# A residual block in split precision: another order of the eleven weight slabs of a pair, other places for the side work, and one more weight sum made by a DMA

## The chip, the cores and the metric

The kernel runs on one core of a Trainium2 chip. The metric is the time of one execution on the device, in microseconds (us); the median of three runs is given. Engines: TensorE (PE; PEld are its weight loads), VectorE (DVE), ScalarE (ACT), GpSimd (POOL) and SyncE (SP). SP issues the plain DMA loads, POOL the DMAs that add to what is in the buffer.

## What is computed

One layer over 256 positions of width 2048, in float32:

```
h = RMSNorm(x);  p = h @ W_in                      # 2048 -> 7168
A = retention over 8 heads (rotary, decay, group norm, gate)
B = chunked attention over 8 heads (QK norm, relative bias)
x = x + concat(A, B) @ W_out                       # 2048 -> 2048
h = RMSNorm(x)
x = x + square(relu(h @ W1)) @ W2                  # 2048 -> 8192 -> 2048
```

The change is in the last line, the feed-forward part.

## The kernel before, in words

**Split precision.** Each float32 weight slab (128 partitions x 2048 elements, 1 MB: four blocks of 128 rows by 512 columns) is split in two halves of the matmul's type: ScalarE copies the raw slab to `w_hi` (`hi_slab`, line 904), VectorE subtracts `w_hi` from the raw slab into `w_lo` (`lo_slab`, line 1244). The activations are split the same way into *forms* (`hF_hi`/`hF_lo` for the up projection, `dF_hi`/`dF_lo` for the down projection). A block product is then three matmuls of 512 columns: hi x hi, hi x lo, lo x hi. `w_hi` and `w_lo` are rings of three slabs, so `hi_slab(s)` waits until the matmuls have used slab s-3 (`slab_used`), and the matmuls of slab s wait for `slab_lo`.

**Fewer products.** The part runs as four rounds; in each, 2048 hidden values are made (up) and used (down). A round has four *pairs* (line 675): two of kind U (up, each with two column groups of 512) and two of kind D (down). Half of the inner dimension of a pair is done by a seven-product scheme instead of eight (sums and differences of blocks of weights and of activations): the steps Q1, P5, P6, Q2, P7, P3, P4, each a `product` of 12 matmuls. The other half is done plainly: the four steps R1 to R4 (`rest`), each of 24 matmuls on one slab. The R steps of a pair are run one pass later, between the products of the next pair; pass p has eleven steps:

```
STEPS = 11
R1, Q1, R2, P5, R3, P6, R4, Q2, P7, P3, P4 = range(STEPS)
```

After P4 comes R1 of the next pass, so the four products Q2, P7, P3, P4 stand in a row.

**Weight sums.** P5, P6, P7 and P4 need sums of the four raw slabs a, b, d and e of the pair. a is read by Q1. Then VectorE adds b to a (`sum_slabs`, line 1252) for P5, and d to it for P6. POOL's DMAs add from HBM: one adds d's weights to the buffer of b (line 453) for P7, released by the first VectorE sum; one adds e's to the buffer of a (line 457) for P4, released by P6's low half. Plain loads of d and e serve P3 and Q2.

**Results.** The products lie in the PSUM banks bX, bF, bH, bY, bZ, bW. `keep_q1` (ScalarE, line 955) copies Q1's result out of bX before P6 may write there; `sum_u1`, `sum_u2`, `sum_u3`, `sum_v4` (VectorE, lines 1350 to 1366) form the partial results. For a U pair the next pass adds them to the banks (`up_sum`, into `hid`), applies ReLU and square on ScalarE (lines 943, 948), and TensorE transposes the hidden values in two halves (`hid_blocks`, line 672; eight transposes each). From them `stage`, `d_mix_of`, `d_hi` and `d_lo` make the eleven forms of the down projection: seven from the first U pair, four from the second. For a D pair `add_products` and `add_bank` add to `xs`, the running x.

**Order.** Nothing is planned at run time: every engine has its list written out by hand in its loop over p, with the side work placed between two slabs. All waits are semaphore counts. The raw slabs lie in five buffers; `raw_plan` (line 303) gives each load the buffer whose last reader comes first, and SP issues the loads in the order of `sources` (line 289), each behind the low half that reads the buffer last (`slab_lo`, line 408).

Of the kernel before, what the change touches and what calls it, by code (L numbers as in the profile page):

```python
# [56 lines left out]
R1, Q1, R2, P5, R3, P6, R4, Q2, P7, P3, P4 = range(STEPS)  # L57
# [7 lines left out]
def hybrid_block(nc, x, x_cols, w_att, w_ret, w_out, w_up, w_down, gains, rel_windows, rope_cos, rope_sin, decay, out):  # L65
# [3 lines left out]
    with ExitStack() as ctx:  # L69
# [176 lines left out]
        b_summed = sem("b_summed")  # L246
        e_summed = sem("e_summed")
# [102 lines left out]
        def added(p):  # L350

            return 2 * OUT_GROUPS + 4 * (2 * (p // 4) + p % 4 - 2)

# [4 lines left out]
        def _(sp):  # L358
# [54 lines left out]
            for c in range(4):  # L413
                for m in range(MT):

                    sp.wait_ge(acc_read_dve, added(PAIRS - 2 + c // 2) + 2 * (c % 2) + m + 1)
                    sp.dma_start(out_rows[:, m, c * N:(c + 1) * N], xs[:, m, c * N:(c + 1) * N]).then_inc(stored, 16)
# [4 lines left out]
        def _(pool):  # L422
# [48 lines left out]
        def _(pe):  # L471
# [148 lines left out]
            def rest(p, step, hi, lo, form, banks, opens, closes):  # L620
# [4 lines left out]
                for m in range(MT):  # L625
# [7 lines left out]
                    if closes and m == 0:  # L633
                        mm.then_inc(half_used, 1)
                mm.then_inc(slab_used, 1)
# [39 lines left out]
            for p in range(PAIRS + 1):  # L675
# [6 lines left out]
                def forms(n):  # L682

                    if up:
                        pe.wait_ge(hF_lo_ok, n)
                    else:
                        pe.wait_ge(dF_lo_ok, FORMS * g + n)
# [9 lines left out]
                else:  # L697
                    rest_forms(9)
                    rest(p, R1, hi_, lo_, REST, (bH, bY), (False, False), False)
                if live:  # L700
                    forms(1)
# [9 lines left out]
                if live:  # L711
                    forms(3)
# [8 lines left out]
                if live:  # L721
                    forms(6)
# [8 lines left out]
                if live:  # L731
                    forms(7)
                    bank_read(pe, prev, 0)
                    product(p, Q2, hi, lo, A12, bH, False)
                    pe.wait_ge(u1_ok, p + 1)
                    product(p, P7, hi, lo, S3N, bX, True)
                    bank_read(pe, prev, 2)
                    product(p, P3, hi, lo, S4, bZ, False)
                    if was_up:
                        hid_blocks(prev, 1)  # L740
                    if prev < 0:
                        x_blocks(OUT_GROUPS - 1)
                    bank_read(pe, prev, 1)
# [4 lines left out]
        def _(act):  # L748
# [135 lines left out]
            def hi_slab(s):  # L884
# [5 lines left out]
                if step in (P5, P6):  # L890
                    act.wait_ge(summed, 2 * p + (P5, P6).index(step) + 1)
# [58 lines left out]
            def keep_q1(p):  # L950

                act.wait_ge(slab_used, slab_no(p, Q1) + 1)
                if p > 0:
                    bank_read(act, p - 1, 0)
                nc.scalar.activation(q1[:], bX[:], ACT.Copy).then_inc(q1_ok, 1)

            def stage(u, n):

                act.wait_ge(hid_tr, 8 * (u // 4) + n + 1)
                nc.scalar.activation(sd[:, n, :], bT[n % 2][:], ACT.Copy).then_inc(d_stage, 1)  # L960
# [8 lines left out]
            for p in range(PAIRS + 1):  # L969
                prev, s = p - 1, STEPS * p  # L970
                was_up, first_up, live = kind(prev) == "U", prev >= 0 and prev % 4 == 0, p < PAIRS
                if not live:
# [7 lines left out]
                if prev % 4 == 1 and prev >= 0:  # L980
                    act.wait_ge(d_mix, 4 * (prev // 4) + 2)
                    d_hi(S1, sd[:, 1, :])
                    d_hi(A12, sd[:, 2, :])
                    d_hi(A22, sd[:, 3, :])

                hi_slab(s + 3)
                if prev % 4 == 1 and prev >= 0:
                    act.wait_ge(d_mix, 4 * (prev // 4) + 3)
                    d_hi(S2N, sd[:, 0, :])
# [5 lines left out]
                if prev % 4 == 1 and prev >= 0:  # L995
                    act.wait_ge(d_mix, 4 * (prev // 4) + 4)
                    d_hi(S4, sd[:, 2, :])

                hi_slab(s + 5)
                keep_q1(p)  # L1000

                hi_slab(s + 6)
                if was_up:
# [5 lines left out]

                hi_slab(s + 7)  # L1010

                hi_slab(s + 8)
                if first_up:
                    stage(prev, 0)
# [5 lines left out]
                hi_slab(s + 9)  # L1020
                if was_up:
                    relu(prev, 0, 1)
                    relu(prev, 1, 1)
                    square(prev, 0, 1)
                    square(prev, 1, 1)
                if first_up:
                    d_hi(A11, sd[:, 0, :])

                hi_slab(s + 10)
                if p == 0:  # L1030
                    stream_squares(OUT_GROUPS - 1)
                if first_up:
                    act.wait_ge(d_mix, 4 * (prev // 4) + 1)
                    d_hi(S3N, sd4[:])

                hi_slab(s + 11)

                hi_slab(s + 12)
                if first_up:
                    stage(prev, 2)  # L1040
                    stage(prev, 3)
                elif was_up:
                    d_rest(prev, 2)
                    d_rest(prev, 3)
# [3 lines left out]
        def _(dve):  # L1048
# [283 lines left out]
            def add_products(p, m, second):  # L1332
# [4 lines left out]
                dve.wait_ge(ready, p + 1)  # L1337
                nc.vector.tensor_tensor(cols, other[:], cols, ALU.add).then_inc(xs_ok, 1)

            def add_bank(p, m, second):  # L1340
# [4 lines left out]
                if p >= 0:  # L1345
                    dve.wait_ge(xs_ok, added(p) - 2 * OUT_GROUPS + 2 * second + m + 1)
# [3 lines left out]
            def sum_u1(p):  # L1350

                dve.wait_ge(slab_used, slab_no(p, P6) + 1)
                dve.wait_ge(q1_ok, p + 1)
                nc.vector.tensor_tensor(u1[:], bX[:], q1[:], ALU.add).then_inc(u1_ok, 1)
# [20 lines left out]

            for p in range(PAIRS + 1):
                prev, s = p - 1, STEPS * p
                kept, live = kind(prev), p < PAIRS
                first_up = prev >= 0 and prev % 4 == 0
                second_up = prev >= 0 and prev % 4 == 1  # L1380
                g = prev // 4
                if not live:
# [4 lines left out]
                    for second in range(2):  # L1387
                        for m in range(MT):
                            add_products(prev, m, second)
                    for second in range(2):  # L1390
                        for m in range(MT):
                            add_bank(prev, m, second)
# [4 lines left out]
                else:  # L1397
                    sum_u2(prev)
# [5 lines left out]
                if second_up:  # L1404
                    dve.wait_ge(d_stage, 4 * g + 4)
                    d_mix_of(sd[:, 1, :], sd[:, 1, :], sd[:, 3, :], ALU.subtract)
                    d_lo(g, 3, S1, sd[:, 1, :])

                lo_slab(s + 3)
                if p > 0:  # L1410
                    sum_v4(prev)
                if second_up:
                    d_lo(g, 4, A12, sd[:, 2, :])
                    d_lo(g, 5, A22, sd[:, 3, :])
                    dve.wait_ge(d_mix, 4 * g + 2)
                    d_mix_of(sd[:, 0, :], sd[:, 1, :], sd[:, 0, :], ALU.subtract)

                sum_slabs(p, "a", "d", ["d"])
                lo_slab(s + 4)
# [3 lines left out]
                if second_up:  # L1423
                    d_lo(g, 6, S2N, sd[:, 0, :])
                    dve.wait_ge(d_mix, 4 * g + 3)
                    d_mix_of(sd[:, 2, :], sd[:, 2, :], sd[:, 0, :], ALU.add)
                if kept == "D":
                    add_products(prev, 0, 0)
                    add_products(prev, 1, 0)

                lo_slab(s + 5)
                if second_up:
                    d_lo(g, 7, S4, sd[:, 2, :])
                if kept == "U":
                    up_sum(prev, 0, 0)
                    up_sum(prev, 1, 0)
                if kept == "D":
                    add_bank(prev, 0, 0)
                    add_bank(prev, 1, 0)

                lo_slab(s + 6)

                lo_slab(s + 7)

                if kept == "D":
                    add_products(prev, 0, 1)
                    add_products(prev, 1, 1)
                sum_u1(p)
                lo_slab(s + 8)
                if kept == "U":  # L1450
                    up_sum(prev, 0, 1)
                else:
                    add_bank(prev, 0, 1)

                lo_slab(s + 9)
                if kept == "U":
                    up_sum(prev, 1, 1)
                else:
                    add_bank(prev, 1, 1)
                if first_up:  # L1460
# [79 lines left out]
```

## Time and profile before

| | us |
|---|---|
| median of three runs | 1175.92 (1172.63 to 1175.97) |
| the profiled execution, its own time | 1176.99 |
| its span | 1175.0 |
| TensorE busy | 1124.2 |
| VectorE busy | 888.5 |
| ScalarE busy | 632.8 |
| mean granted TensorE clock | 0.988 of full |
| HBM read | 250.37 MB |

A busy time is the time in which the engine has an instruction under way; the matmuls overlap each other by some tenths of a microsecond, so a busy TensorE may still be slowed. The feed-forward part begins near 421 us and ends with the span; the first D pair of the second round is the pass called pair 6 (passes count from 0). In the timeline a row is: start, length, engine, line, operation, output<-inputs, shapes, count, and in brackets how long the engine had been idle and what released it.

### The profile page before, as it was taken

What the parts mean: (1) busy time and instruction counts of PE and PEld (TensorE: products, weight loads), DVE (VectorE), ACT (ScalarE), POOL (GpSimd) and SP (SyncE); (2) the same over time, 40 slices, a digit from 0 to 9 for tenths busy, and PEclk for the clock granted to TensorE, in tenths of its full rate; (3) what the DMA queues carried; (4) which work ended last, traced back from release to release, by engine and by line L of the source; (5) the groups of instructions that cost most, each with busy time, mean ns of one, the idle gap of its engine ahead of it and who ended that gap; (6) DMA issues with size and microseconds to landing.
All of it is one profiled execution on the core that took longest, in us unless ns stands there. A gap on an engine that the chain in (4) does not pass through costs nothing.

```text
span 1175.0 us, 13700 instructions
## 1 busy us (share of the span) xinstructions
PE 1124.2 (96%) x5234; PEld 948.8 (81%) x5234; DVE 888.5 (76%) x924; ACT 632.8 (54%) x717; POOL 53.4 (5%) x58
## 2 busy tenths in 40 slices
PE   8999999999999999988999998999998999997998
PEld 8889889989988878776788876788876788876787
DVE  6667667657657678786898877888876889877885
ACT  6545445445454556556555555555565554574652
POOL 0000000000000000100000000000000000000000
PEclk9999999999999999999999998999999999999999
DMA  9745445445455467866688765688866788875692
GB/s 358 303 165 195 161 169 191 166 148 207 165 195 180 179 215 250 231 198 214 193 266 282 228 218 183 213 281 248 238 232 166 224 294 230 265 238 139 232 259 100
DMA packets 39551, 253.14 MB, mean 215 GB/s; under 512 B 4432, under 2 KB 4944, under 8 KB 12624
## 3 DMA queue, kind: packets, MB, share of 16 engines
q1 hardware_dynamic: 34896, 218.93, 50.7%
q0 software_dynamic: 4608, 33.56, 15.4%
q8 instruction: 33, 0.54, 0.2%
q14 instruction: 14, 0.11, 0.0%
HBM read 250.37 MB, written 2.10 MB: 215 GB/s over the span
## 4 chain that ended last, share of the span: by engine, by line
PE 75%; DVE 11%; ACT 8%; issue 3%; DMA 2%; SPq 0%; ACTq 0%; DVEq 0%
PE acc L485 10%; PE acc L487 10%; PE acc L486 10%; PE acc L628 8%; PE acc L631 8%; PE acc L630 8%; DVE w_lo L1244 6%; ACT w_hi L904 5%; PE bankC L614 2%; PE bankC L616 2%; PE bankC L615 2%; PE acc L614 2%; PE acc L616 2%; PE acc L615 2%; DMA raw<-in_w_ret 1%
## 5 line engine op out<-in xcount | busy, mean ns | idle before, releaser
L1244 DVE TENSOR_TENSOR w_lo<-raw,w_hi 128x2048 fp32r<-128x2048 f32 x180 | 411.4, 2288 | 120.9 <-ACT w_hi L904 120.9
L904 ACT ACTIVATE w_hi<-raw 128x2048 fp32r<-128x2048 f32 x180 | 342.3, 1912 | 193.7 <-PE acc L631 120.2
L1051 DVE TENSOR_TENSOR w_lo<-raw,w_hi 128x1024 fp32r<-128x1024 f32 (+1 forms) x152 | 167.6, 1107 | 67.1 <-ACT w_hi L756 67.0
L485 PE MATMUL acc<-w_hi,hT_hi 128*128 128x512 f32 (+1 forms) x512 | 191.6, 374 | 2.9 <-DVE w_lo L1051 2.9
L487 PE MATMUL acc<-w_hi,hT_lo 128*128 128x512 f32 (+1 forms) x512 | 185.7, 363 | 0.0
L486 PE MATMUL acc<-w_lo,hT_hi 128*128 128x512 f32 (+1 forms) x512 | 185.5, 362 | 0.0
L756 ACT ACTIVATE w_hi<-raw 128x1024 fp32r<-128x1024 f32 (+1 forms) x152 | 142.8, 963 | 33.8 <-PE acc L487 27.5
L628 PE MATMUL acc<-w_hi,hF_hi 128*128 128x512 f32 x256 | 103.6, 405 | 15.3 <-DVE w_lo L1244 14.3
L485 PEld LDWEIGHTS acc<-w_hi,hT_hi 128*128 128x128 f32 x512 | 96.3, 188 | 13.2 <-DVE w_lo L1051 3.8
L487 PEld LDWEIGHTS acc<-w_hi,hT_lo 128*128 128x128 f32 x512 | 96.1, 188 | 10.2
L486 PEld LDWEIGHTS acc<-w_lo,hT_hi 128*128 128x128 f32 x512 | 96.4, 188 | 9.5
L631 PE MATMUL acc<-w_hi,hF_lo 128*128 128x512 f32 x256 | 101.9, 398 | 0.0
L630 PE MATMUL acc<-w_lo,hF_hi 128*128 128x512 f32 x256 | 101.6, 397 | 0.0
L628 PE MATMUL acc<-w_hi,dF_hi 128*128 128x512 f32 x256 | 100.0, 391 | 0.1
L630 PE MATMUL acc<-w_lo,dF_hi 128*128 128x512 f32 x256 | 99.7, 390 | 0.0
L631 PE MATMUL acc<-w_hi,dF_lo 128*128 128x512 f32 x256 | 99.6, 389 | 0.0
L1252 DVE TENSOR_TENSOR raw<-raw 128x2048 f32<-128x2048 f32 x32 | 73.0, 2282 | 0.0
L628 PEld LDWEIGHTS acc<-w_hi,hF_hi 128*128 128x128 f32 x256 | 49.5, 193 | 27.8 <-issue 16.5
L631 PEld LDWEIGHTS acc<-w_hi,hF_lo 128*128 128x128 f32 x256 | 49.2, 192 | 10.8
L630 PEld LDWEIGHTS acc<-w_lo,hF_hi 128*128 128x128 f32 x256 | 49.7, 194 | 10.1
L628 PEld LDWEIGHTS acc<-w_hi,dF_hi 128*128 128x128 f32 x256 | 48.2, 188 | 10.9 <-issue 0.9
L631 PEld LDWEIGHTS acc<-w_hi,dF_lo 128*128 128x128 f32 x256 | 48.2, 188 | 10.1
(191 smaller groups left out, 1716.4 us busy)
## 6 DMA issues: line engine op xcount, KB each, us to landing
raw<-in_w_up SPq DMA_DIRECT2D x64, 1024.0 KB, 6.1
raw<-in_w_down SPq DMA_DIRECT2D x64, 1024.0 KB, 5.0
raw<-in_w_ret SPq DMA_DIRECT2D x32, 1024.0 KB, 4.8
raw<-in_w_att SPq DMA_DIRECT2D x28, 768.0 KB, 4.3
raw<-in_w_out SPq DMA_DIRECT2D x16, 1024.0 KB, 4.9
raw<-in_w_up POOLq DMA_DIRECT2D x16, 1024.0 KB, 8.6
raw<-in_w_down POOLq DMA_DIRECT2D x16, 1024.0 KB, 8.8
raw<-in_w_att SPq DMA_DIRECT2D x8, 384.0 KB, 7.2
```

Of the source, the lines that this page charges most:

```text
L485: nc.tensor.matmul(o, hi[:, k, tile_cols(m)], wh, start=first, stop=False)
L486: nc.tensor.matmul(o, hi[:, k, tile_cols(m)], wl, start=False, stop=False)
L487: mm = nc.tensor.matmul(o, lo[:, k, tile_cols(m)], wh, start=False, stop=last)
L614: nc.tensor.matmul(bank[:], hi[:, form, tile_cols(t)], wh[:, cols], start=t == 0, stop=False)
L628: nc.tensor.matmul(banks[m][:], hi[:, form + m, tile_cols(t)], wh[:, cols], start=opens[m] and t == 0, stop=False)
L630: nc.tensor.matmul(banks[m][:], hi[:, form + m, tile_cols(t)], wl[:, cols], start=False, stop=False)
L631: mm = nc.tensor.matmul(banks[m][:], lo[:, form + m, tile_cols(t)], wh[:, cols], start=False, stop=closes and t == SLAB_KT - 1)
L756: nc.scalar.activation(piece(w_hi, q, 0, PIECE_KT * n), raw[:, q // 2, (q % 2) * PIECE_KT * n:(q % 2 + 1) * PIECE_KT * n], ACT.Copy).then_ ...
L904: nc.scalar.activation(w_hi[:, ring(s)], raw[:, r, :], ACT.Copy).then_inc(slab_hi, 1)
L1051: nc.vector.tensor_tensor(piece(w_lo, q, 0, PIECE_KT * n), raw[:, q // 2, (q % 2) * PIECE_KT * n:(q % 2 + 1) * PIECE_KT * n], piece(w_hi, ...
L1244: nc.vector.tensor_tensor(w_lo[:, ring(s)], raw[:, r, :], w_hi[:, ring(s)].bitcast(f32), ALU.subtract).then_inc(slab_lo, 1)
L1252: nc.vector.tensor_tensor(raw[:, r, :], raw[:, r, :], raw[:, q, :], ALU.add).then_inc(summed, 1)
```

## The change

The order of the steps becomes R1, Q1, R2, P5, Q2, R3, P6, R4, P7, P3, P4. In the list of loads e comes before d. The sum for P6 (d added to the buffer of a) is no longer made by VectorE but by a third POOL DMA, released by P5's low half. The second half of a U pair's transposes moves from before P4 to the middle of R1 of the next pass, and with it the side work of ScalarE and VectorE moves to other slabs; the bank is added to x before the first two product sums, and the order of waits follows.

```diff
-R1, Q1, R2, P5, R3, P6, R4, Q2, P7, P3, P4 = range(STEPS)
+R1, Q1, R2, P5, Q2, R3, P6, R4, P7, P3, P4 = range(STEPS)
...
-                order += [(p, "d")] if p < PAIRS else []
+                order += [(p, "e"), (p, "d")] if p < PAIRS else []
                 order += [(p - 1, "R3"), (p - 1, "R4")]
-                order += [(p, "e")] if p < PAIRS else []
...
+        X_FORMS = {Q1: 1, P5: 3, Q2: 4, P6: 6, P7: 6, P3: 7, P4: 7}
+        D_FORMS = {Q1: 1, P5: 3, Q2: 3, P6: 4, P7: 5, P3: 6, P4: 7}
... POOL, add_slabs(p)
-                pool.wait_ge(summed, 2 * p + 1)
+                pool.wait_ge(summed, p + 1)
                 row = ((first + 1) * SLABS + 1) * P
                 nc.gpsimd.dma_start(raw[:, PLAN[p, "b"][0], :], table[row:row + P, :],
                                     accum_op=ALU.add).then_inc(b_summed, 16)
+                pool.wait_ge(slab_lo, slab_no(p, P5) + 1)
+                nc.gpsimd.dma_start(raw[:, PLAN[p, "a"][0], :], table[row:row + P, :],
+                                    accum_op=ALU.add).then_inc(d_summed, 16)
                 pool.wait_ge(slab_lo, slab_no(p, P6) + 1)
... TensorE
-                    rest(p, R1, hi_, lo_, REST, (bH, bY), (False, False), False)
+                    rest(p, R1, hi_, lo_, REST, (bH, bY), (False, False), False,
+                         (lambda: hid_blocks(p - 2, 1)) if kind(p - 2) == "U" else None)
...
+                    forms(Q2)
+                    bank_read(pe, prev, 0)
+                    product(p, Q2, hi, lo, A12, bH, False)
                 if prev < 0:
                     rest_out(R3, 2)
...
-                    if was_up:
-                        hid_blocks(prev, 1)
... ScalarE, hi_slab(s)
-                if step in (P5, P6):
-                    act.wait_ge(summed, 2 * p + (P5, P6).index(step) + 1)
+                if step == P5:
+                    act.wait_ge(summed, p + 1)
+                elif step == P6:
+                    act.wait_ge(d_summed, 16 * p + 16)
... ScalarE, pass p (new list)
                 hi_slab(s + 2)
+                if held_first:
+                    stage(p - 2, 2, A12)
+                    stage(p - 2, 3)
+                if held_second:
+                    d_rest(p - 2, 2)
+                    d_rest(p - 2, 3)
                 hi_slab(s + 3)
+                if held_first:
+                    act.wait_ge(d_mix, 4 * g + 1)
+                    d_hi(S1, sd4[:])
...
+                hi_slab(s + 6)
+                if held_first:
+                    act.wait_ge(d_mix, 4 * g + 3)
+                    d_hi(S2N, sd[:, 0, :])
+                hi_slab(s + 7)
                 keep_q1(p)
                 if was_up:
                     relu(prev, 0, 0)
                     relu(prev, 1, 0)
                     square(prev, 0, 0)
                     square(prev, 1, 0)
+                if held_first:
+                    d_hi(S3N, sd[:, 1, :])
                 hi_slab(s + 8)
+                hi_slab(s + 9)
...
+                hi_slab(s + 10)
                 if was_up:
                     relu(prev, 0, 1)
+                hi_slab(s + 11)
+                if was_up:
                     relu(prev, 1, 1)
+                hi_slab(s + 12)
+                if was_up:
                     square(prev, 0, 1)
                     square(prev, 1, 1)
... VectorE, pass p (new list)
+                    sum_u3(prev)
                     sum_u2(prev)
                 sum_slabs(p, "a", "b", ["b"])
                 lo_slab(s + 2)
+                if p > 0:
+                    sum_v4(prev)
+                if held_first:
                     dve.wait_ge(d_stage, 4 * g + 4)
+                    d_mix_of(sd4[:], sd[:, 1, :], sd[:, 3, :], ALU.subtract)
+                    d_lo(g, 2, A12, sd[:, 2, :])
+                if held_second:
+                    d_lo(g, 10, REST + 2, bT[0][:])
+                    d_lo(g, 11, REST + 3, bT[1][:])
                 lo_slab(s + 3)
-                sum_slabs(p, "a", "d", ["d"])
...
                 lo_slab(s + 4)
+                if p > 0:
+                    read_first(prev)
+                lo_slab(s + 5)
+                if was_down:
+                    add_products(prev, 0, 0)
...
+                lo_slab(s + 7)
+                if was_down:
+                    add_products(prev, 1, 0)
+                    add_products(prev, 0, 1)
+                    add_products(prev, 1, 1)
...
+                lo_slab(s + 8)
                 sum_u1(p)
                 lo_slab(s + 9)
+                for m in range(MT):
+                    up_sum(prev, m, 1) if was_up else add_bank(prev, m, 1)
+                if held_first:
+                    d_lo(g, 6, S4, sd[:, 2, :])
+                    d_lo(g, 7, A22, sd[:, 3, :])
...
```

`held_first` is the first D pass of a round, `held_second` the second; `read_first` is the two `up_sum` or `add_bank` of the first column group.

## Rows read from the trace of the kernel before

**Rows 1.** The page, part 1: busy us, share of the span, instructions of each engine.
```profile
PE 1124.2 (96%) x5234; PEld 948.8 (81%) x5234; DVE 888.5 (76%) x924; ACT 632.8 (54%) x717; POOL 53.4 (5%) x58
```

**Rows 2.** Windows by pair: length, busy by engine, granted clock, DMA share, GB/s.
```profile
606.00:646.80 40.80, 40.80 (x181) 33.78 (x181) 36.28 (x26) 21.60 (x12) 1.73 (x2) 1.00 0.83 259
646.80:692.10 45.30, 42.80 (x197) 35.29 (x197) 35.04 (x24) 28.61 (x26) 1.73 (x2) 1.00 0.73 225
692.10:747.00 54.90, 48.08 (x198) 38.34 (x198) 42.40 (x33) 30.16 (x29) 1.73 (x2) 0.91 0.65 204
747.00:787.80 40.80, 40.80 (x181) 33.75 (x181) 36.01 (x28) 21.59 (x12) 1.73 (x2) 1.00 0.79 248
...
927.20:968.30 41.10, 41.04 (x182) 33.69 (x181) 37.53 (x28) 21.61 (x12) 1.73 (x2) 1.00 0.84 268
```

**Rows 3.** Timeline of TensorE in pairs 5 and 6.
```profile
685.61 0.60 PE L672 MATMUL bankA<-ident,hid 128*128 128x128 f32 x4
686.05 0.60 PE L672 MATMUL bankB<-ident,hid 128*128 128x128 f32 x4
689.14 0.47 PE L614 MATMUL acc<-w_hi,hF_hi 128*128 128x512 f32 x1 [2.50 <-DVE w_lo L1244]
...
713.39 0.76 PE L628 MATMUL acc<-w_hi,hF_hi 128*128 128x512 f32 x1 [3.64 <-DVE w_lo L1244]
...
742.40 0.47 PE L614 MATMUL acc<-w_hi,dF_hi 128*128 128x512 f32 x1 [1.99 <-DVE w_lo L1244]
```

**Rows 4.** Window around the stop before R3 of pair 6.
```profile
705.50:721.60 16.10, 11.54 (x39) 8.71 (x38) 12.74 (x13) 5.93 (x6) 0.86 (x1) 0.79 0.36 120
```

**Rows 5.** Timeline of ScalarE, pairs 4 and 5.
```profile
624.87 0.60 ACT L955 ACTIVATE q<-bankC 128x512 f32<-128x512 f32 x1 [3.27 <-DVE xs L1348]
...
638.72 1.92 ACT L904 ACTIVATE w_hi<-raw 128x2048 fp32r<-128x2048 f32 x1 [0.80 <-PE acc L616]
641.44 1.92 ACT L904 ACTIVATE w_hi<-raw 128x2048 fp32r<-128x2048 f32 x1 [0.80 <-PE bankC L616]
...
682.58 0.72 ACT L943 ACTIVATE hid<-hid,rstd 128x512 f32<-128x512 f32 x1 [2.35 <-DVE hid L1330]
```

**Rows 6.** Timeline of VectorE, pairs 4 and 6.
```profile
607.61 0.68 DVE L1362 TENSOR_TENSOR u<-bankC,u 128x512 f32<-128x512 f32 x1
608.21 2.28 DVE L1252 TENSOR_TENSOR raw<-raw 128x2048 f32<-128x2048 f32 x1
610.40 2.28 DVE L1244 TENSOR_TENSOR w_lo<-raw,w_hi 128x2048 fp32r<-128x2048 f32 x1
...
643.39 2.29 DVE L1244 TENSOR_TENSOR w_lo<-raw,w_hi 128x2048 fp32r<-128x2048 f32 x1 [0.35 <-ACT w_hi L904]
...
708.37 2.28 DVE L1252 TENSOR_TENSOR raw<-raw 128x2048 f32<-128x2048 f32 x1
710.95 2.29 DVE L1244 TENSOR_TENSOR w_lo<-raw,w_hi 128x2048 fp32r<-128x2048 f32 x1 [0.30 <-ACT w_hi L904]
```

**Rows 7.** Landings: issues at 612.72 (SP), 620.79 (SP), 610.78 and 624.47 (POOL).
```profile
raw<-in_w_down SPq DMA_DIRECT2D x1, 1024.0 KB, 8.6
...
raw<-in_w_up SPq DMA_DIRECT2D x1, 1024.0 KB, 5.8
...
raw<-in_w_up POOLq DMA_DIRECT2D x1, 1024.0 KB, 9.0
...
raw<-in_w_up POOLq DMA_DIRECT2D x1, 1024.0 KB, 8.0
```

**Rows 8.** Timeline of the two DMA issues of 610 to 613.
```profile
610.78 0.86 POOL L453 DMA_DIRECT2D raw<-in_w_up  x1 [26.25 <-DVE raw L1252]
...
612.72 0.33 SPq L411 DMA_DIRECT2D raw<-in_w_down  x1
```

**Rows 9.** DMA queues in 606 to 646.8: packets, MB, share of 16 engines.
```profile
q1 hardware_dynamic: 1158, 8.44, 54.9%
q0 software_dynamic: 288, 2.10, 27.5%
```

More of the change, by code:

```diff
@@ L618, in product, with rest @@
                 mm.then_inc(slab_used, 1)
-            def rest(p, step, hi, lo, form, banks, opens, closes):
+            def rest(p, step, hi, lo, form, banks, opens, closes, between=None):
                 s = slab_no(p, step)
@@ L634, in rest @@
                         mm.then_inc(half_used, 1)
+                    if between and m == 0:
+                        between()
                 mm.then_inc(slab_used, 1)
@@ L711, in _ @@
                 if live:
-                    forms(3)
+                    forms(P5)
                     if p > 0:
@@ L721, in _ @@
                 if live:
-                    forms(6)
+                    forms(P6)
                     pe.wait_ge(q1_ok, p + 1)
@@ L952, in keep_q1, with stage @@
                 act.wait_ge(slab_used, slab_no(p, Q1) + 1)
-                if p > 0:
+                if kind(p - 1) == "U":
                     bank_read(act, p - 1, 0)
+                elif kind(p - 1) == "D":
+                    act.wait_ge(xs_ok, products_added(p - 1) + 1)
                 nc.scalar.activation(q1[:], bX[:], ACT.Copy).then_inc(q1_ok, 1)
-            def stage(u, n):
+            def stage(u, n, form=None):
                 act.wait_ge(hid_tr, 8 * (u // 4) + n + 1)
+                if form is not None:
+                    d_hi(form, bT[n % 2][:])
                 nc.scalar.activation(sd[:, n, :], bT[n % 2][:], ACT.Copy).then_inc(d_stage, 1)
@@ L970, in _ @@
                 prev, s = p - 1, STEPS * p
-                was_up, first_up, live = kind(prev) == "U", prev >= 0 and prev % 4 == 0, p < PAIRS
-                if not live:
+                was_up = kind(prev) == "U"
+                fresh_first = prev >= 0 and prev % 4 == 0
+                held_first, held_second = p >= 2 and p % 4 == 2, p >= 2 and p % 4 == 3
+                g = (p - 2) // 4
+                if p == PAIRS:
                     for s in range(STEPS * PAIRS + 2, SLABS_ALL):
@@ L1337, in add_products @@
                 dve.wait_ge(ready, p + 1)
+                if not second:
+                    dve.wait_ge(acc_read_dve, added(p) + m + 1)
                 nc.vector.tensor_tensor(cols, other[:], cols, ALU.add).then_inc(xs_ok, 1)
@@ L1344, in add_bank @@
                 bank_done(p, m, second)
-                if p >= 0:
-                    dve.wait_ge(xs_ok, added(p) - 2 * OUT_GROUPS + 2 * second + m + 1)
+                if p >= 0 and second:
+                    dve.wait_ge(xs_ok, products_added(p) + 2 + m + 1)
                 bank = ((bH, bY), (bZ, bW))[second][m]
@@ L1353, in sum_u1 @@
                 dve.wait_ge(q1_ok, p + 1)
+                if kind(p - 1) == "D":
+                    dve.wait_ge(xs_ok, products_added(p - 1) + 2)
                 nc.vector.tensor_tensor(u1[:], bX[:], q1[:], ALU.add).then_inc(u1_ok, 1)
@@ L1386, in _ @@
                     lo_slab(s + 3)
[L1387 to L1392, printed above, removed]
+                    read_first(prev)
[3 more added lines that the diff above has]
+                    add_products(prev, 1, 1)
+                    add_bank(prev, 0, 1)
+                    add_bank(prev, 1, 1)
                     break
@@ L1397, in _ @@
                 else:
+                    sum_u3(prev)
                     sum_u2(prev)
@@ L1463, in _ @@
-                if second_up:
-                    d_lo(g, 8, REST, bT[0][:])
-                    d_lo(g, 9, REST + 1, bT[1][:])
+                lo_slab(s + 8)
+                sum_u1(p)
+                lo_slab(s + 9)
+                for m in range(MT):
+                    up_sum(prev, m, 1) if was_up else add_bank(prev, m, 1)
+                if held_first:
+                    d_lo(g, 6, S4, sd[:, 2, :])
+                    d_lo(g, 7, A22, sd[:, 3, :])
+                if fresh_first:
+                    dve.wait_ge(d_stage, 4 * (prev // 4) + 1)
+                    d_lo(prev // 4, 1, A11, sd[:, 0, :])
@@ L1467, in _ @@
                 lo_slab(s + 10)
-                if first_up:
-                    d_lo(g, 2, S3N, sd4[:])
+                if fresh_second:
+                    d_lo(prev // 4, 8, REST, bT[0][:])
+                    d_lo(prev // 4, 9, REST + 1, bT[1][:])
                 lo_slab(s + 11)
-                sum_u3(p)
                 lo_slab(s + 12)
@@ L1476, in _ @@
                     x_stage_rest(OUT_GROUPS - 1)
-                if second_up:
-                    d_lo(g, 10, REST + 2, bT[0][:])
-                    d_lo(g, 11, REST + 3, bT[1][:])
 def tables():
```

133 lines of the change are left out of this document (46 added, 87 removed).

## The prediction

> **What bounds the kernel now.** The page first: TensorE is busy 96% of the span, VectorE 76%, ScalarE 54% [rows 1]. So a gain can only come from time in which TensorE stands, or runs at its lower clock, in the feed-forward part. I cut that part into its pairs (one pass of the loop of eleven slabs) with the windows. Pairs 4 and 7 take 40.8 us with TensorE busy for all of it; pair 5 takes 45.3 and pair 6 takes 54.9 [rows 2]. A pair has 180 matmuls, so one takes 40.8/180 = 0.227 us: 2.72 for a product (12 matmuls), 5.43 for an ordinary slab (24). Four pairs take 787.8 - 606.0 = 181.8 and the next four 968.3 - 787.8 = 180.5 [rows 2], mean 181.15. The floor is 4 x 40.8 = 163.2 plus the transposes of the hidden values, four times two blocks of 0.44 [rows 3], 0.9 each time: 166.8. About 14.3 per four pairs is loss.
>
> Where it is: TensorE stands before the fourth product in a row, for the low half of its slab (2.5 us at 689.1, 2.0 at 742.4), and in pair 6 before R3 (3.6 at 713.4) [rows 3]. In front of those low halves VectorE does other 2.2 us sums and 0.6 us form work. Behind the stop before R3 the granted clock of 705.5 to 721.6 is 0.79, the lower level of 1.2 GHz for a part of it [rows 4]; pair 6 as a whole has 0.91 [rows 2].
>
> **The rhythm.** A slab's high half (ScalarE) can start when the slab three before it is used; 641.44 to the end of the low half at 645.68 is 4.24 us [rows 5, 6], 4.34 with the hand-over, and 0.15 until the matmul starts. Two products in front give 5.44, so 0.9 less hand-overs is the whole slack; two slabs of which one is ordinary give 8.15. I follow one new pass from T, the start of R1's first matmul.
>
> **VectorE.** Removed: one `sum_slabs` (2.28 us, 2.2 back to back) per pair [rows 6]. In pair 4 it lies in a pass without a stop, so removing it gives nothing there; in pair 6 it stands ahead of the low half of R3: it begins at 708.37, and the low half that R3 waits for follows at 710.95 [rows 6]. The form work of that pair (`d_mix`, `d_lo`) moves beside R1, R2, R3 and R4, `sum_u3` moves to the head of the pass. By row, in pair 4 (T = 605.8) the order u2, sum, low half of R2 ends at 612.7, T+6.9 [rows 6]; with `sum_u3` ahead T+7.5. R2 is wanted at T+8.15: hidden. P5's low half ends about T+10.3 (8.1 after `sum_v4`, then 2.2), wanted at T+13.6. In the pass that makes the down forms (pair 6's kind): sum_u3, sum_u2, sum, R2's low half, v4, mix, A12, low half P5 (its high half waits for R1, used at T+6.35 with the transposes now inside R1), S1, mix, low half Q2, two bank reads, low half R3. Added up with 0.6 and 2.2 the last ends at T+19.9, for a slab wanted at T+19.9: 0.1 to 0.4 late. From R4 on in the same pass: low half P3, two bank reads, S4, A22, low half P4, two rest forms, low half of the next R1: 34.5 + 2.2 + 1.2 + 1.2 + 2.2 + 1.2 + 2.2 = T+44.7, wanted T+44.1: 0.7 late. In the pass after it `d_lo` 10 and 11 come after sum, R2 and v4, at T+9.45, and R2's matmuls wait for them from T+9.05: 0.55 late. The other passes have no VectorE stop. Without any DMA trouble four pairs then need 166.8 + 0.7 + 0.55 = 168.05.
>
> **ScalarE.** In pair 5 the stop before P4 has its cause here: the high half of P4's slab stands behind the second ReLU, which begins at 682.58 after 2.35 us of waiting for VectorE's hidden sum [rows 5], and behind the squares. The change puts one ReLU behind the high half of P4, one behind that of the next R1, the squares behind that of the next Q1, and makes the sums both ready before: that wait is gone, and 0.6 to 1.2 us beside slabs with over 2 us to spare are hidden. So the 3.6 us stop of pair 5 (45.3 - 40.8 - 0.9) goes whole. If this cover failed, 0.7 to 1.4 us per up pass would come back.
>
> **Loads by SP.** The new order Q2 before R3 takes a raw buffer early, and the loads shift: by the rule that gives the buffer longest free, R3 is now loaded into the buffer that R2's low half frees, R4 into Q2's. Before, R3's load went out at about R1's low half, and R4's at R2's. So the load of R3 is issued at T+7.5 and its high half may start at T+13.6 (R2 used), 6.1 us later. The trace has a load in exactly this place, the one at 612.72, 1.9 us behind the POOL accumulate of 610.78: it took 8.6 us to land, where a load that has no accumulate beside it took 5.8 (620.79) [rows 7, 8]. It waits until the accumulate (9.0) has left the DMA engines. So R3 lands at T+16.1, 0.06 + 4.24 + 0.15 later its matmuls start, T+20.55, instead of T+19.0: 1.5 us of stop in the two up passes, 0.4 in the form pass, 0.1 after it. Bounds: 0 (5.8 us) and 2.9 (10 us). I take 1.5 because the row is the same constellation.
>
> **The new accumulate "d".** It replaces the sum on VectorE. It is released by P5's low half, T+10.3, and its result is the slab of P6. On its queue "b" is ahead: issued at T+5.5 and, by the row, landed 9.0 later, T+14.6. An accumulate lands in 8.0 (that of 624.47) or 9.0, beside a load [rows 7]; its packets take 27.5% of 40.8 us for two, 5.6 each, plain loads 54.9% for eight, 2.8 each [rows 9]. Order in the engines: b, R3's load (issued before d), d, R4's load: d at 16.1 + 5.6 = T+21.7, R4 at T+24.5. ScalarE takes them in order: high half P6 at 21.8, high half R4 24.6 to 26.5, then `keep_q1`, which the change puts behind R4 (0.5 [rows 5]), and P6's matmuls wait for it: T+27.1, where R3 ends at T+26.0. That is 1.1 at most; where packets overlap it is 0. I take 0.7 in three passes and 0.9 in the form pass, 3.0 for four. "e" is released by P6's low half, T+26, lands in 8.0 to 9.0, T+34 to 35, and is wanted at T+35: hidden, with no room left (before, the one released at 624.5 had landed at 632.5, and its high half began at 638.72 [rows 5]).
>
> The Trainium skill, "DMA: Bandwidth & Descriptors", section "Queues, rings and completion order", says that an engine goes round between its rings and changes only at packet borders, a packet being some 9 to 17 descriptors. By that R3's load gets its turn between b and d, as assumed; the trace agrees so far that the load of 612.72 did not interleave with the accumulate, and no row shows two accumulates in a row.
>
> **Cost at nothing.** More bytes: a third accumulate of 5.6 brings the 82.4% of 40.8 us to 96% [rows 9], 39.2 us of a 43.7 us pair, 90%. Splitting the transposes (`hid_blocks` second half into R1 of the next pass) moves 0.9, does not remove it; its squares are ready about T+0.3, the transposes want them at T+2.7. SP issues its eight loads in order, each behind the low half that frees its buffer; of those only R3's has a release (R2's low half) so near its use, and R2's own load is released by P3's low half of the pass before, 9 us ahead of its use, so no load holds the next one up. The end (last R4, one add, one store) is the same work; the products are added earlier.
>
> **Sum.** 168.05 + (1.5 + 1.5 + 0.4 + 0.1) + 3.0 = 174.6 for four pairs against 181.15: 6.6 less, times four 26. The profiled execution's own time is 1177.0 (span 1175.0); that gives 1151, and as the median shown is 1.1 lower, 1150.
>
> **The rivals.**
> A: the transfers are in time: R3's load slips in beside the accumulate, and d follows early enough. Then 168.05 stands, 13.1 less per four, 52 in all: 1125. For it: a load alone landed in 5.8. Against: the 8.6 row. Chance 0.17.
> B: crowding. Three accumulates at 90% of the DMA engines make R3, d and e later by another 1 to 1.6 us in each pair: 16 to 26 us, 1166 to 1176. For it: 83% of the engines is taken already in the undisturbed pair [rows 2]. Chance 0.16, a fifth of it within 0.3%.
> C, the slower side: d reaches the ring while b is still running (released at T+10.3, b lands at T+14.6), and the engines finish both before R3's load has its turn: 14.6 + 5.6 + 2.8 = T+23.0, R3 starts at T+27.45, late by 8.4, 8.4, 7.5 and 7.0. Four pairs 168.05 + 31.3 = 199.4, 18.2 more than now, 1176 + 73 = 1250, and more where the clock falls behind such a stop as it did behind the stop of 713.4 [rows 3, 4]. It decides from where the stops before R3 and P6 together pass (181.15 - 168.05)/4 = 3.3 us a pair; I have 1.6. For it: a plain load did wait for the whole of an accumulate. Against: R3's load is issued 3 us ahead of d. Chance 0.17, with milder forms of it.
>
> **Numbers.** Forecast 1150 (its own range 1138 to 1162), chance 0.50; A 0.17, B 0.16, C 0.17. A difference under 0.3% (3.5 us) can't be told from none. Faster: 0.50 + 0.17 + 0.13 = 0.80; same 0.03; slower 0.17. The range reaches down past A, since the VectorE stops of 1.25 might also be hidden, to 1118, and up over B to 1180; it leaves out most of C.
>
> **What would show it.** Right: no stop before P4 but in the form pass; a stop of 1 to 2 us before R3 ended by the low half, with ScalarE's high half of R3 released by the DMA and not by TensorE; a smaller one before P6 ended by ScalarE's `keep_q1` or by the low half; pairs of 43, 44, 45 and 43 us; granted clock near 1.00 throughout. Wrong: R3's load landing in under 6 us (A), landing after d (C), or stops before P4 for "e" (B). The sum of 26 would be wrong in kind, not only in size, if pair 6 still took over 50 us.

## The result and the profile after

The changed kernel takes 1184.67 us (median of six runs, 1178.31 to 1188.18), the one before 1174.57 in six runs. The ratio is 1.0083, 95% interval [1.0053, 1.0113]: 10 us slower, where 26 us faster was forecast. The profiled execution is the fastest of the six, 1178.31 with a span of 1176.5, so what it shows is a little better than the usual run.

The page, parts 1, 3 and 4 (engines; queues; the chain that ended last), against [rows 1]:

```profile
PE 1121.6 (95%) x5234; PEld 943.6 (80%) x5234; DVE 853.9 (73%) x908; ACT 632.2 (54%) x717; POOL 67.2 (6%) x74
...
q1 hardware_dynamic: 34896, 218.93, 49.6%
q0 software_dynamic: 6912, 50.33, 22.0%
...
PE 50%; DVE 21%; DMA 19%; ACT 7%; issue 2%; POOL 0%; SPq 0%; ACTq 0%; DVEq 0%
```

The chain that ended last in the kernel before:

```profile
PE 75%; DVE 11%; ACT 8%; issue 3%; DMA 2%; SPq 0%; ACTq 0%; DVEq 0%
```

VectorE has lost 34.6 us of work, as it should (16 sums), and TensorE's busy time has hardly changed (2.6 us less). New is the 19% of DMA in the chain that ended last; before it was 2%. The waits of the changed kernel between 510 and 1160 us name the place (us in total, times, longest):

```profile
DVE w_lo L1267 <- ACT w_hi L922: 129.0, 69, 6.0
ACT w_hi L922 <- DMA raw<-in_w_down: 98.4, 19, 8.2
ACT w_hi L922 <- DMA raw<-in_w_up: 76.4, 16, 7.7
...
PE acc L640 <- DVE w_lo L1267: 24.3, 16, 3.8
```

ScalarE's high halves wait for DMAs, VectorE's low halves for the high halves, TensorE for the low halves. Windows by pair, 4 to 8 (against [rows 2]):

```profile
607.60:651.80 44.20, 41.24 (x181) 33.64 (x181) 34.04 (x25) 21.48 (x12) 2.59 (x3) 1.00 0.85 261
651.80:696.80 45.00, 42.00 (x190) 34.55 (x189) 32.67 (x22) 26.95 (x23) 2.59 (x3) 1.00 0.86 264
696.80:741.50 44.70, 43.10 (x196) 34.90 (x194) 38.18 (x33) 30.89 (x31) 2.59 (x3) 1.00 0.83 255
741.50:786.00 44.50, 42.95 (x190) 34.70 (x191) 35.99 (x27) 22.61 (x15) 2.59 (x3) 1.00 0.83 256
786.00:832.30 46.30, 42.54 (x181) 34.83 (x180) 34.39 (x25) 21.47 (x12) 2.59 (x3) 0.96 0.85 258
```

The pair of 54.9 us is now 44.7 and the stop before P4 is gone (one of 1.4 us is left, in pair 11). But every pair takes 44 to 47 us (pair 1, told of below, 52), those of 40.8 us included. Four pairs (607.6 to 786.0) take 178.4; the next four end at 969.6, 183.6. TensorE's timeline has the stops: before R3 in pairs 5 and 8, before P6 in pair 7.

```profile
673.80 0.47 PE L640 MATMUL acc<-w_hi,hF_hi 128*128 128x512 f32 x1 [3.00 <-DVE w_lo L1267]
...
769.31 0.47 PE L626 MATMUL bankC<-w_hi,dF_hi 128*128 128x512 f32 x1 [1.15 <-DVE w_lo L1267]
...
808.71 0.77 PE L640 MATMUL acc<-w_hi,dF_hi 128*128 128x512 f32 x1 [3.76 <-DVE w_lo L1267]
```

Behind the last one the matmul took 0.77 us, and pair 8 has a mean granted clock of 0.96, a part of it at the lower level, 1.2 GHz: TensorE loses 1.6 us more there than the stop itself. The same happened behind the stops before R3 of pairs 10 (2.3 us) and 13 (3.2), and not behind those of pairs 4, 5, 9 and 12 (2.4 to 3.0). From issue to landing, the loads of R3 in pairs 5 and 8 (issued at 659.01 and 793.16) and the accumulate d of pair 8 (796.22) take, in us:

```profile
raw<-in_w_up SPq DMA_DIRECT2D x1, 1024.0 KB, 10.4
...
raw<-in_w_down SPq DMA_DIRECT2D x1, 1024.0 KB, 11.1
...
raw<-in_w_up POOLq DMA_DIRECT2D x1, 1024.0 KB, 12.8
```

And one long stop, once: in pass 1 POOL has its power for the second norm (L474) ahead of b's accumulate (L462), which goes out at 477.63, 13.0 us into the pass instead of 5 to 6; d is queued right behind it and lands 15.5 us later, and P6 stands 6.9 us.

```profile
474.97 2.69 POOL L474 TENSOR_TENSOR rstd<-me,neg_half 128x2 f32<-128x2 f32 x1 [26.58 <-DVE me L1334]
477.63 0.89 POOL L462 DMA_DIRECT2D raw<-in_w_up  x1
478.22 1.19 POOL L465 DMA_DIRECT2D raw<-in_w_up  x1
...
498.17 0.76 PE L626 MATMUL bankC<-w_hi,hF_hi 128*128 128x512 f32 x1 [6.85 <-DVE w_lo L1267]
```

### The profile page after: what moved, and what is told of

The parts are those of the page before. It is cut to its first block, busy times and chain, and to the rows that moved or that the text cites. A ratio compares the mean times of both kernels' runs of the same rounds, so it can differ in the third digit from the quotient of the medians.

```text
span 1176.5 us, 13704 instructions
## 1 busy us (share of the span) xinstructions
PE 1121.6 (95%) x5234; PEld 943.6 (80%) x5234; DVE 853.9 (73%) x908; ACT 632.2 (54%) x717; POOL 67.2 (6%) x74
## 4 chain that ended last, share of the span: by engine, by line
PE 50%; DVE 21%; DMA 19%; ACT 7%; issue 2%; POOL 0%; SPq 0%; ACTq 0%; DVEq 0%
DVE w_lo L1267 13%; DMA raw<-in_w_down 10%; PE acc L497 10%; PE acc L499 10%; PE acc L498 10%; DMA raw<-in_w_up 7%; ACT w_hi L922 5%; PE acc L640 3%; PE acc L643 3%; PE acc L642 3%; DVE raw L1275 3%; PE bankC L626 2%; PE bankC L628 2%; PE bankC L627 2%; DVE dF_lo L1397 1%
## 5 line engine op out<-in xcount | busy, mean ns | idle before, releaser
L640 PE MATMUL acc<-w_hi,dF_hi 128*128 128x512 f32 x256 | 102.1, 399 | 11.0 <-DVE w_lo L1267 10.1
L643 PEld LDWEIGHTS acc<-w_hi,hF_lo 128*128 128x128 f32 x256 | 48.9, 191 | 10.6
L643 PEld LDWEIGHTS acc<-w_hi,dF_lo 128*128 128x128 f32 x256 | 48.4, 189 | 10.4
L642 PEld LDWEIGHTS acc<-w_lo,dF_hi 128*128 128x128 f32 x256 | 48.5, 189 | 9.5
```

The source lines that it names most:

```text
L640: nc.tensor.matmul(banks[m][:], hi[:, form + m, tile_cols(t)], wh[:, cols], start=opens[m] and t == 0, stop=False)
L642: nc.tensor.matmul(banks[m][:], hi[:, form + m, tile_cols(t)], wl[:, cols], start=False, stop=False)
L643: mm = nc.tensor.matmul(banks[m][:], lo[:, form + m, tile_cols(t)], wh[:, cols], start=False, stop=closes and t == SLAB_KT - 1)
```

## The experiments

Three theories are tried. An accumulate is a POOL DMA that adds to what is in the buffer: b is the one into b's buffer (for P7), d the one that adds d to a's buffer (for P6), e the one that adds e to it (for P4). T is the start of R1's first matmul in a pass. Theory 1: the accumulates hold the DMA engines while R3's and R4's loads and d itself are wanted; where each stands in the queues makes the time. Theory 2: the side work in its new places costs. Theory 3: the bytes as such. Each kernel was timed in four to ten executions beside the kernel before, which took 1174.6 to 1175.1.

**The two parts of the change, each alone.** e1 keeps the new order and makes the sum on VectorE again:

```diff
 VectorE, behind lo_slab(s + 3):
+                sum_slabs(p, "a", "d", ["d"])
 POOL, add_slabs:
-                pool.wait_ge(slab_lo, slab_no(p, P5) + 1)
-                nc.gpsimd.dma_start(raw[:, PLAN[p, "a"][0], :], table[row:row + P, :],
-                                    accum_op=ALU.add).then_inc(d_summed, 16)
```

> The new order of steps, loads and side work, but the sum a+d is made by VectorE again (2.2 us beside P5's slab) and the third accumulate is gone. Theory 1 (the accumulates of b and d push the loads of R3 and R4 and d itself back in the DMA engines): without d the load of R3 lands after 8.6 us instead of 10.4 to 11.2, the stop before R3 falls from 3.2 to about 1.5 in the up passes, the one before P6 vanishes, the form pass gains 2.2 us of VectorE work: 4 pairs about 174 instead of 181, in all about 1150. Theory 2 (the side work in its new places is what costs): stops before R3 and P6 stay or grow by the 2.2 us per pair, 1185 to 1215. Theory 3 (the bytes as such bound the part): the third accumulate's share goes, about 1160, but the loads land late all through the pass, not only those of R3 and R4.

Measured: 1138.65 us, ratio 0.969 [0.9674, 0.9706]. Theory 1's direction, with 11 us more than it expected. R3's load of pair 5 lands after

```profile
raw<-in_w_up SPq DMA_DIRECT2D x1, 1024.0 KB, 8.5
```

and TensorE's timeline has only this stop left in that pair:

```profile
654.69 0.47 PE L637 MATMUL acc<-w_hi,hF_hi 128*128 128x512 f32 x1 [1.11 <-DVE w_lo L1262]
```

So the order and the moved side work are worth 36 us, and making the sum by the third accumulate instead of on VectorE takes away 46. Theory 2 falls here: the side work stands in its new places in e1 too. e2 is the other part alone, on the kernel before:

```diff
-                sum_slabs(p, "a", "d", ["d"])          (VectorE)
+                pool.wait_ge(slab_lo, slab_no(p, P5) + 1)
+                nc.gpsimd.dma_start(raw[:, PLAN[p, "a"][0], :], table[row:row + P, :],
+                                    accum_op=ALU.add).then_inc(d_summed, 16)
```

> The kernel before with one thing changed: d is added to a's buffer by a POOL DMA released by P5's low half, the order of steps stays. P6 is then two steps behind P5, its high half may start 3.9 us after P5's low half, and the accumulate takes 9 to 10 us from its release. Theory 1 expects a stop of 5 to 6 us before P6 in every pair, some 60 to 90 us in all: 1230 to 1260. Theory 2 (VectorE's time is what the kernel lacks) expects a gain of up to 2.2 us in the pairs with stops, below 1174.

Measured: 1283.92 us, ratio 1.0925 [1.0907, 1.0943]: 109 us slower, more than expected, pairs of 48 to 59 us. The direction is theory 1's. The expectation took 9 to 10 us for d; outside the form passes it lands 11.9 to 13.1 us after its issue (14.8 in pair 1). The row of pair 4 shows a second part:

```profile
661.37 0.76 PE L618 MATMUL bankC<-w_hi,hF_hi 128*128 128x512 f32 x1 [7.00 <-ACT q L961]
```

P6's low half ended at 659.98; P6 waits 1.4 us more for `keep_q1`, which in the old list waits for an addition that VectorE does behind that low half. And the mean granted clock is 0.956: the slower matmuls behind the stops cost some 26 us more than in the kernel before.

**Which accumulate does what.** Two kernels that leave one out, and so compute with a weight sum that lacks a slab:

```diff
 e3: -  the DMA d;  hi_slab of P6 waits: act.wait_ge(summed, p + 1)
 e4: -  the DMA b;  hi_slab of P7 waits: act.wait_ge(summed, p + 1)
```

> The changed kernel without the accumulate of d: P6 and P4 then work on sums that lack d's weights. Everything else as changed. Theory 1: R3's load lands after about 8.6 us (b alone in front), stop before R3 about 1.5 in up passes and 0.4 in the form pass, none before P6; 4 pairs 168 to 172, in all 1120 to 1140. Theory 2: the stops before R3 and P6 stay near 3.2 and 1.5, above 1165.

Measured: 1136.39 us, ratio 0.9671 [0.9655, 0.9687]. R3's load of pair 5:

```profile
raw<-in_w_up SPq DMA_DIRECT2D x1, 1024.0 KB, 8.6
```

> The changed kernel without the accumulate of b: P7 then works on a sum that lacks one slab's weights. d is now alone on its queue. Theory 1 (b is what R3's load waits for first): R3's load lands in 5 to 6 us, no stop before R3; d is released at T+10.0, lands 9 us later at about T+19.3 instead of T+22.7, so its high half is only 3 us behind R2's use and P6 starts on time or 0.5 late: 1115 to 1135, lower than without d. If d were the one that holds R3's load up, the load would still land after 8 to 10 us.

Measured: 1128.72 us, ratio 0.961 [0.9594, 0.9626]. The same load:

```profile
raw<-in_w_up SPq DMA_DIRECT2D x1, 1024.0 KB, 4.7
```

The load takes 4.7 us with nothing before it, 8.6 behind b, 10.4 with d behind it as well, though d is issued 3 us after the load. Both effects are now shown. The queues show how. For 4 us behind b the load moves next to nothing, with or without d (one packet of q1, SP's queue, against 83 or 87 of q0, POOL's). In its last stretch it shares the DMA engines with d, and without d has them for itself. The first two lines are 666 to 669.4 us of the changed kernel, the third is 648.8 to 650.4 of e3 (packets, MB, share of 16 engines):

```profile
q0 software_dynamic: 62, 0.51, 73.0%
q1 hardware_dynamic: 68, 0.43, 33.3%
...
q1 hardware_dynamic: 92, 0.62, 97.7%
```

So it takes both: with b left out, d goes out 3.3 us behind the load just the same and the load still lands in 4.7. The other passes bear this out. Where d follows the load by 3.1 or 3.2 us (the up passes), the changed kernel's load takes 1.3 to 2.3 us longer than e3's (0.1 in pair 12); where d follows by 4.3 us (the D passes), only 0.1 to 0.8. e3 is only 2 us faster than e1: making the sum on VectorE is nearly free in the new order.

**POOL's order in pass 1.** In e5 the power stands behind pair 1's accumulate of b.

> The changed kernel with one thing moved: POOL's power for the second norm no longer stands in front of the accumulate of b of pair 1, it comes behind it. In the changed kernel that accumulate is issued 12.8 us into pass 1 instead of 5, d of pair 1 lands 28.9 us into the pass and P6 stands 8.6 us. Expected by theory 1: that stop falls to 1 to 3 us, 6 to 8 us in all, about 1177. If it stays, POOL's order was not its cause.

Measured: 1181.85 us (ten runs, 1175.67 to 1188.32), ratio 1.0058 [1.0034, 1.0083]. Pass 1 falls from 52.3 to 47.7 us and its stop before P6 from 6.9 to 1.6, but the total differs from the changed kernel by less than the runs spread. The cause of the stop is right, its weight in the total can't be read.

**Other places for the same transfers.** e6 changes only the list of loads, e7 only POOL's list:

```diff
 e6, sources(p):
-                order += [(p, "e"), (p, "d")] if p < PAIRS else []
+                order += [(p, "e")] if p < PAIRS else []
                 order += [(p - 1, "R3"), (p - 1, "R4")]
+                order += [(p, "d")] if p < PAIRS else []
 e7, add_slabs(p): d's wait and DMA first, then b's
```

> The changed kernel with another order of loads: R3, R4, d instead of d, R3, R4. R3's load is then released by R1's low half (some 8 us earlier), R4's by R2's, and d's plain load, which is wanted 18 us later, by Q2's. No accumulate and no byte less. Theory 1: the stop before R3 vanishes (32 us in all, less what reappears before P6, since d's accumulate still lands at about T+22: P6 then stands 2 to 2.5 us a pair): 1160 to 1172. Theory 3 (bytes): the loads land as late as before and the time stays near 1184.

Measured: 1185.91 us, ratio 1.0081 [1.0049, 1.0113]. The stop before R3 is gone in every pair, and P6's has grown to 1.6 to 4.3 us (6.9 in pair 1, 1.3 in pair 0): nothing gained. The expectation of 1160 to 1172 was wrong. d lands no earlier, and with R3 on time the wait for it comes out in full before P6. What ended P6's waits between 510 and 1160 us (us in total, times, longest):

```profile
PE bankC L627 <- DVE w_lo L1268: 23.6, 10, 4.3
...
PE bankC L627 <- DVE dF_lo L1398: 11.8, 4, 3.2
```

That is P6's low half, and in the form passes (2, 6, 10, 14) a form of the down projection that ScalarE makes behind P6's high half.

> The changed kernel with the accumulates of b and d swapped on POOL's queue: d first, released by P5's low half as before, b behind it (P7 wants it some 8 us after P6 wants d). Same bytes. Theory 1: between R2's low half and the issue of d the engines are free, R3's load lands in under 6 us, in time; d has nothing in front and lands at about T+19.3; P6 is at most 0.5 to 1 late; b lands at about T+26 to 28, in time or just late for P7: 1128 to 1145, as fast as without b's accumulate. Theory 3 (bytes): no better than 1175.

Measured: 1209.13 us, ratio 1.0271 [1.0228, 1.0314], the largest miss. d did land in time (pair 8: 8.7 us after its issue, T+19.2). But R4's load is now behind both accumulates and takes 12.6 us, and ScalarE has it before `keep_q1` (L974), without which P6 may not start. ScalarE, then TensorE, of pair 8:

```profile
832.83 1.91 ACT L921 ACTIVATE w_hi<-raw 128x2048 fp32r<-128x2048 f32 x1 [4.12 <-DMA raw<-in_w_down]
834.65 0.58 ACT L974 ACTIVATE q<-bankC 128x512 f32<-128x512 f32 x1
...
835.33 0.76 PE L625 MATMUL bankC<-w_hi,hF_hi 128*128 128x512 f32 x1 [3.12 <-issue]
```

The matmul starts right behind the copy. So the place of `keep_q1` behind R4's high half, part of the change, is a second mechanism. e9 moves it alone, e10 in e7, e11 in e7 with e6's loads, e12 adds e5's edit to e11:

```diff
                 hi_slab(s + 6)
+                keep_q1(p)
 ...
                 hi_slab(s + 7)
-                keep_q1(p)
```

> The changed kernel with keep_q1 moved on ScalarE from behind R4's high half to behind P6's. P6's matmuls need it, R4's high half does not precede them otherwise. In the changed kernel P6's low half and keep_q1 end within 0.3 us of each other (both hang on the accumulate of d), so theory 1 expects almost nothing here: 1178 to 1184. If keep_q1's place were a cost of its own in the changed kernel: below 1165.

Measured: 1186.86 us, ratio 1.0114 [1.0077, 1.015]. No gain (a little above the top of the expected range, 1184, within the spread of the changed kernel's runs): in the changed kernel itself this place costs nothing, d is as late.

> The kernel with d's accumulate ahead of b's (e7), and keep_q1 behind P6's high half. In e7 d landed at T+19 to 20, in time, and still P6 stood 3.4 to 8 us: ScalarE had R4's high half in front of keep_q1, and R4's load waited for both accumulates until T+26.4. Expected: no stop before P6; R4's own matmuls now wait for that load, 26.4 + 4.3 against T+27.2 or 28.1: 2.7 to 3.6 a pair, so about 1170 to 1180, 30 to 40 below e7.

Measured: 1177.55 us, ratio 1.0031 [1.0013, 1.005]: 32 below e7, as expected; the stops moved from P6 to R4 or to the transposes before it.

> The kernel of e10 with the order of loads of e6 as well (R3 and R4 before d, so R4's load is released by R2's low half and has no accumulate in front). Still three accumulates and all bytes. Theory 1 (places in the queues, not bytes and not side work): no stop before R3, P6 or R4 over 1 us, 1122 to 1135, below both kernels. Theory 3 (bytes, DMA engines some 95% taken): above 1150.

Measured: 1156.97 us, ratio 0.9852 [0.983, 0.9874]. Below both kernels, but 22 us above the expected range's end. No stop is left before R3, and hardly one before P6 or R4; it has moved to P4. Pair 5: e's accumulate, issued at 664.98 behind b, lands in 13.0 us, its high half waits for it, and P4 stands.

```profile
raw<-in_w_up POOLq DMA_DIRECT2D x1, 1024.0 KB, 13.0
...
677.96 1.92 ACT L922 ACTIVATE w_hi<-raw 128x2048 fp32r<-128x2048 f32 x1 [4.82 <-DMA raw<-in_w_up]
...
682.35 0.47 PE L626 MATMUL acc<-w_hi,hF_hi 128*128 128x512 f32 x1 [1.50 <-DVE w_lo L1267]
```

Its window for pair 5 has 0.86 of the DMA engines busy. Theory 1 in its strict form (places only) is not borne out: with three accumulates per pair one of them was late in every order tried. Theory 3's "above 1150" holds, but that the bytes as such are the limit is not shown: b, issued 0.5 us behind d, takes 15.5 us, and e stands behind b on the same queue. Whether the order on POOL's one queue or the DMA engines' total is what holds e back was not separated.

> The kernel of e11 with POOL's power moved as in e5, behind both accumulates of pair 1. Expected 4 to 8 us less than e11 if the one long stop of pair 1 is still there, else the same.

Measured: 1156.23 us, ratio 0.9835 [0.9818, 0.9852]: the same as e11.

**Two accumulates, well placed.** e8 is e1 with b released later:

```diff
 POOL, add_slabs(p):
-                pool.wait_ge(summed, 2 * p + 1)
+                pool.wait_ge(slab_lo, slab_no(p, P5) + 1)
```

> The order-only kernel (sum a+d on VectorE, two accumulates) with b's accumulate released by P5's low half (T+10.2) instead of by the first sum (T+5). Theory 1: R3's load lands in under 6 us, the stops before R3 (16 us in all there) go, b lands at about T+20 for a slab wanted at T+25: 1120 to 1126. Theory 2 (side work bounds it): stays at 1138.

Measured: 1125.3 us, ratio 0.9579 [0.9552, 0.9606]: the best of all, 49 us below the kernel before. R3's load of pair 5 lands in 4.7 us, there is no stop before R3, P6 or P4 over 0.1 us, and the windows of four pairs are these:

```profile
593.40:634.20 40.80, 40.80 (x181) 33.80 (x181) 36.37 (x26) 21.59 (x12) 1.73 (x2) 1.00 0.83 258
634.20:675.90 41.70, 41.70 (x189) 34.62 (x189) 34.74 (x23) 27.01 (x23) 1.72 (x2) 1.00 0.79 252
675.90:719.20 43.30, 42.98 (x197) 35.25 (x197) 40.88 (x34) 31.15 (x31) 1.72 (x2) 1.00 0.79 243
719.20:761.40 42.20, 42.03 (x189) 34.55 (x189) 37.74 (x28) 22.89 (x15) 1.72 (x2) 1.00 0.80 250
```

Together 168.0 us.

## Why the prediction was wrong

- **Where the kernel before lost its time, and that the new order cures it: right.** The stops before P4 and the long form pass went. e8, in which no transfer is late, takes 168.0 us for four pairs, where the prediction worked out 168.05 "without any DMA trouble", and its rival A, 1125, is near e8's 1125.3. That the numbers agree so closely is in part luck: e8 still makes the sum on VectorE, which the 168.05 had taken out. The VectorE steps that were called late stand in the profile of the changed kernel, smaller: 0.3 us before R2 of pair 7 and 0.3 before its R1, where 0.55 and 0.7 were forecast.
- **The load of R3: right mechanism, wrong size. This step carries most of the error.** The prediction took 8.6 us from the row with the "same constellation" and so 1.5 us of stop in the up passes. It landed after 10.1 to 11.1 us there, and TensorE stood 2.4 to 3.8 us before R3 (pairs 4, 5, 8, 9, 12, 13; mean 3.0). The constellation was not the same: in the trace of before no second accumulate was behind. e3 (8.6) and the changed kernel (10.4) differ in d alone. The sentence "Order in the engines: b, R3's load, d, R4's load" failed at its second step: the load does wait for b, but d's packets start before the load is done. R3's stops cost some 31 us over the part, 5 of them by the lower clock behind those of pairs 8, 10 and 13, against 14 forecast.
- **The accumulate of d: the time is near, one place was missed.** T+21.7 was forecast, T+22.4 to 23.9 measured in pairs 2 to 15; the stops before P6 cost some 21 us in all, against 12. Of these, 8.5 lie in pass 1 alone (the stop of 6.9 and the lower clock behind it). That was missed: POOL's list was not followed past its power instruction. Before, the same late issue cost little, as only P7 hung on it. In the form passes it is not the low half or `keep_q1` that ends P6's wait but a form made behind P6's high half (0.7 to 1.3 us).
- **The sum of the errors.** 17 us of R3 and 9 of P6 are 26 of the 27 us between the 1151 that the prediction gave a profiled execution and the measured 1178.3.
- **The break-even was right.** The prediction put it at 3.3 us a pair before R3 and P6; the measured 31 + 21 us are 3.3 a pair, and the profiled execution is 1.3 us slower than that of before. The other executions are slower by 4 to 10 us more. On record is that they ran more at the lower clock: mean granted 0.982 to 0.988 against 0.993, which times their spans gives 1162 to 1167 us against 1168. Added waiting at full clock would have raised that product, so the surplus goes with the clock. Why more stops were followed by the lower level in them is open; no trace of them was kept.
- **The rivals.** The outcome is nearest to B, crowding, and worse than it was priced (up to 1176): R3's load and d came later than forecast. B's own sign, stops before P4 for e, stands in pair 11 alone. C's mechanism, both accumulates before the load, did not occur: the load landed before d, at T+17.8 in pair 5 against d's T+22.9.
- **"e hidden, with no room left": right** for the changed kernel (at most 1.5 us lost before P4, in pair 11), and e is what came late in e11.
- **`keep_q1` behind R4: priced together with d, at 0.7.** In the changed kernel moving it gains nothing (e9); it is what made e7 32 us slower than e10.
- **The Trainium skill**, "DMA: Bandwidth & Descriptors", section "Queues, rings and completion order", has an engine go round its rings by packets of some 9 to 17 descriptors. It was read as if R3's load would be done before d begins. By the landings (8.6 without d, 10.4 with it) the turns do not protect a load issued 3 us ahead; the measurement decides.

## What to carry to other kernels

A transfer's time is a property of what else is in the queues at that moment; take it from a row only if the change leaves the whole neighbourhood as it is, and price it again if another transfer is added behind it, not only before it. Moving work from an engine with slack to a DMA that reads memory a second time is no saving: here the 2.2 us sums on a VectorE that was 76% busy cost some 2 us in all to keep (e1 against e3), and the DMA that replaced them cost 46. When a change has two parts, find the point in time at which each part's transfers are wanted, and release those wanted late, late: delaying b by 5 us was worth 13 us.

## What the runs showed of the hardware

From issue to landing, in pairs 2 to 15:

- A plain 1 MB load lands in 4.7 to 4.9 us with nothing in front (e4), 8.4 to 10.0 when issued 1.9 us behind one accumulate (e1, e3), 10.1 to 11.1 when a second accumulate is also issued 3.1 us behind it, 8.8 to 10.6 when that one comes 4.3 us behind, and 12.3 to 13.8 behind two (e7).
- An accumulate of 1 MB lands in 7.8 to 9.4 us in the kernel before, in 10.8 to 13.5 when issued 5 to 6 us behind another one (d in the changed kernel), and in 15.5 to 16.8 when issued 0.5 us behind another (b in e7). By [rows 9] one of its 8 KB packets takes some 0.62 us of a DMA engine, one of a plain load 0.31.
- Two accumulates per pair leave the DMA engines 0.79 to 0.83 busy and no transfer late (e8); with three they are 0.82 to 0.86 busy and one is late in every order tried. The two ranges touch, so the share alone does not tell whether a transfer will be late.
- Of seven stops of 2.3 to 3.8 us before R3 in the changed kernel, three (2.3, 3.2 and 3.8) were followed by a stretch at the lower clock, which cost 1.6 to 1.7 us each, and four (2.4 to 3.0) were not.
- What is open: why R3's load takes longest in some pairs (11.1 us in pair 8); in e1 and e3 it is so for pairs 8 and 12 too (9.7 to 10.0).
